# Moving the sums of prepared weight rows from GpSimd to VectorE in a two-layer decoder trunk

## The chip, the cores and the metric

The program runs on one core of one Trainium2 chip. The metric is the device time of one execution in microseconds (us); the lower, the better.

## The reference

The input x is 1024 positions by 1024 features in float32. Layer 0 mixes with an mLSTM (4 heads), layer 1 with sliding-window attention over a shared K/V. Behind each mixer stand an output projection and a SwiGLU feed-forward network, which holds most of the work:

```python
def swiglu(x, w_gate_up, w_down):
    gu = x @ w_gate_up
    g, u = jnp.split(gu, 2, axis=-1)
    return (jax.nn.silu(g) * u) @ w_down
...
x = x + swa_sink_mixer(...)   # or mlstm_mixer, whose last step is h @ w_out
x = x + swiglu(rmsnorm(x, ffn_norm[l]), w_gate_up[l], w_down[l])
```

D_FF is 2816, so that w_gate_up has 1024 x 5632 numbers and w_down 2816 x 1024 in each layer. All of it is float32.

## The kernel before

**Arithmetic.** A float32 number is split into a high part (fp32r) and a low part (the rest), and a product is three matmuls: high by high, high by low, low by high. The large products are also made by a scheme with 7 products of half-sized blocks in place of 8 (NQ = 7). For that, each operand comes in 7 "forms", q = 0 to 6. Some forms are plain blocks b11, b12, b21, b22, others are one of four sums (differences) of blocks: s1 = b12 - b11, s2 = b22 - b12 (written over b12), s3 = b22 - s1, s4 = b21 - s3 (written over b11). Form 1 is split from s1, form 2 from s3, form 4 from s2 and form 6 from s4; forms 0, 3 and 5 need no sum. ScalarE makes the high part of a form (a copy), VectorE the low part (a subtraction, whole form less high part).

**Items.** `run(l)` on each engine walks the items of layer l: 8 "out" items, 22 "up" items (one tile of 128 gate and up columns each; the first of them is plain), 20 "down" items. An item makes 7 products, q = 0 to 6; in an up item each has 12 matmuls. Every engine has a queue of its own, written out by hand in the same loops over items and q, and works through it in order; semaphores join them. The up items with their local numbers 10 to 27 are where this change lies.

**An up item.** TensorE makes product q from the resident forms of x and the matrices `mats`, which come from the streamed weight: GpSimd makes the four sums of the stream two items ahead (`stream_sums`, lines 1068 to 1085), ScalarE the high parts for the next item (L1332), VectorE the low parts of q = 0, 3 and 6 (L1853), GpSimd those of q = 1, 2, 4 and 5 (L1090). The products end in PSUM banks that are used again within the item, so they are emptied at once: ScalarE copies those of q = 0, 1, 2 (L1415, L1420, L1423); VectorE adds those of q = 3, 4, 5 (L1896, L1899, L1902) and makes the two hidden halves at q = 6 (L1908). Product 6 goes into the bank that the addition at q = 4 reads, so TensorE waits for L1899 in front of it:

```python
done, count = ((u_act, 5 * k + 1), (u_act, 5 * k + 3), (u_act, 5 * k + 2), (u_dve, 5 * k + 2)
               )[(2, 4, 5, 6).index(q)]
```

**Preparing rows.** Beside this work the up items prepare the rows of the weights that the following items need (w_down, and layer 1's w_out): 12 rows in layer 0, 11 in layer 1. SyncE loads a row's two raw tiles into one of two buffers (`load_prep`, L826), the four sums are made in place and in two small tiles (`prep_sums`, lines 1044 to 1065), ScalarE makes the high part (`prep_hi_of`, L1311), VectorE the low part (`prep_lo_of`, L1832), and SyncE stores the form in HBM (L831). The table `prep_at` says at which (item, q) a form is made: the 84 or 77 forms of a layer are spread evenly over the 126 products of its items 10 to 27. So in layer 0 forms fall on two of three products, and the pattern repeats every three items:

```python
events = [(runs[l][8 + f].n, q) for f in range(2, 20) for q in range(NQ)]
...
prep_at.setdefault(events[k * len(events) // forms_here], []).append((j0 + k // NQ, k % NQ))
```

In VectorE's queue the order within one q of an up item is: the emptying step (`up_out`), the streamed low parts, the prepared low part.

## Time and profile before

| | us |
|---|---|
| median of 3 runs | 1994.05 (1993.57 to 1995.02) |
| profiled execution | 1993.69 |
| its span | 1991.70 |
| TensorE busy | 1971.0 |
| VectorE busy | 1309.1 |
| ScalarE busy | 921.8 |
| GpSimd busy | 1206.0 |

The span runs from the first to the last instruction on the core; the execution's time is 1.99 us more. Busy times are of one profiled execution. A wait in the profile is put down to the instruction that came last before the waiting one started.

### The profile page before, as it was taken

Reading aid. Unit: us, or ns where it says so; the run is one execution under the profiler, and the core shown is the slowest. Engines: PE = TensorE matmul, PEld = TensorE weight load, DVE = VectorE, ACT = ScalarE, POOL = GpSimd, SP = SyncE. Lnnn points to the kernel's source line nnn. Section 1 sums busy time; section 2 is a strip of 40 time slices with the busy share of each in tenths; the row PEclk is TensorE's granted clock in tenths of the full one; section 3 lists DMA queues with packets and bytes.
Section 4 is the critical chain, followed back from the end, with each engine's and each line's share of the span. In section 5 each row is a group of like instructions: output and inputs, shape, how many; then the busy total and the mean of one; then the engine's idle time right before and its main releaser. Section 6 shows DMA issues by size and latency. Waiting matters only on the chain.

```text
span 1991.7 us, 28791 instructions
## 1 busy us (share of the span) xinstructions
PE 1971.0 (99%) x9987; PEld 1654.9 (83%) x9987; DVE 1309.1 (66%) x1743; ACT 921.8 (46%) x1929; POOL 1206.0 (61%) x1055
## 2 busy tenths in 40 slices
PE   8999999999999999999999999999999999999998
PEld 8898988888888888888888878788888888888886
DVE  6665552688777777564665677779776676645567
ACT  6534333376555555432245465457445444432233
POOL 4443322657988988656664112474988888746566
PEclk9999999999999999999999999999999999999999
DMA  7574545835877778695853123553667757597683
GB/s 209 179 249 169 168 156 208 308 120 169 273 245 240 245 244 254 237 390 186 274 181 75 43 86 107 184 186 117 230 227 231 250 204 263 193 356 265 217 265 132
DMA packets 292627, 414.99 MB, mean 208 GB/s; under 512 B 38128, under 2 KB 215304, under 8 KB 292496
## 3 DMA queue, kind: packets, MB, share of 16 engines
q1 hardware_dynamic: 257792, 307.61, 47.2%
q10 hardware_dynamic: 33280, 100.94, 14.1%
q0 software_dynamic: 1424, 4.77, 0.7%
q8 instruction: 73, 1.20, 0.2%
q14 instruction: 58, 0.48, 0.1%
HBM read 259.09 MB, written 154.17 MB: 207 GB/s over the span
## 4 chain that ended last, share of the span: by engine, by line
PE 89%; DVE 4%; POOL 2%; issue 2%; ACT 1%; DMA 1%; SPq 0%; POOLq 0%; ACTq 0%; DVEq 0%
PE ps L2516 21%; PE ps L2518 21%; PE ps L2517 21%; PE ps L2427 9%; PE ps L2429 5%; PE ps L2892 1%; PE ps L2736 1%; PE ps L2737 1%; PE ps L2733 1%; DVE mats L1853 1%; PE ps L2571 1%; PE ps L2866 1%; DVE forms L1952 1%; PE ps L2777 1%; PE ps L2902 1%
## 5 line engine op out<-in xcount | busy, mean ns | idle before, releaser
L2516 PE MATMUL ps<-forms,mats 128*128 128x512 f32 x2016 | 787.8, 391 | 5.9 <-DVE X L1876 1.8
L2518 PE MATMUL ps<-forms,mats 128*128 128x512 f32 x2016 | 784.9, 389 | 0.0
L2517 PE MATMUL ps<-forms,mats 128*128 128x512 f32 x2016 | 784.6, 389 | 0.0
L1090 POOL TENSOR_TENSOR mats<-sum_a,mats 128x256 fp32r<-128x256 f32 (+2 forms) x384 | 407.3, 1066 | 346.9 <-ACT mats L1332 346.2
L2516 PEld LDWEIGHTS ps<-forms,mats 128*128 128x128 f32 x2016 | 378.5, 188 | 89.5 <-issue 10.2
L2518 PEld LDWEIGHTS ps<-forms,mats 128*128 128x128 f32 x2016 | 378.5, 188 | 78.8
L2517 PEld LDWEIGHTS ps<-forms,mats 128*128 128x128 f32 x2016 | 378.6, 188 | 77.6
L1876 DVE TENSOR_TENSOR X<-ps,X 128x512 f32<-128x512 f32 x390 | 267.9, 689 | 188.6 <-PE ps L2518 186.8
L1332 ACT ACTIVATE mats<-sum_a 128x256 fp32r<-128x256 f32 (+2 forms) x392 | 201.2, 516 | 310.8 <-PE ps L2518 289.5
L1853 DVE TENSOR_TENSOR mats<-stream_raw,mats 128x256 fp32r<-128x256 f32 (+2 forms) x302 | 276.5, 918 | 25.9 <-ACT mats L1332 25.1
L1332 ACT ACTIVATE mats<-stream_raw 128x256 fp32r<-128x256 f32 (+2 forms) x302 | 156.4, 519 | 245.2 <-PE ps L2518 240.4
L1832 DVE TENSOR_TENSOR prep_forms<-prep_raw,prep_forms 128x512 fp32r<-128x512 f32 x115 | 156.2, 1358 | 68.6 <-ACT prep_forms L1311 67.8
L1076 POOL TENSOR_TENSOR sum_a<-stream_raw 128x256 f32<-128x256 f32 (+2 forms) x96 | 112.3, 1170 | 108.7 <-DVE mats L1853 55.9
L2427 PE MATMUL ps<-xT_hi,w_split 128*128 128x512 f32 x400 | 166.4, 416 | 0.0
L2427 PE MATMUL ps<-xT_lo,w_split 128*128 128x512 f32 x400 | 156.2, 391 | 0.0
L2429 PE MATMUL ps<-xT_hi,w_split 128*128 128x512 f32 x400 | 134.4, 391 | 0.0
L1077 POOL TENSOR_TENSOR sum_a<-stream_raw 128x256 f32<-128x256 f32 (+2 forms) x96 | 119.8, 1248 | 0.0
L1081 POOL TENSOR_TENSOR sum_a<-sum_a,stream_raw 128x256 f32<-128x256 f32 (+2 forms) x96 | 115.6, 1205 | 0.0
L1085 POOL TENSOR_TENSOR sum_a<-stream_raw,sum_a 128x256 f32<-128x256 f32 (+2 forms) x96 | 111.0, 1157 | 6.9
L1042 POOL TENSOR_TENSOR raw<-raw,gain_cols 128x1024 f32<-128x1024 f32 x31 | 67.9, 2201 | 38.9 <-DMA raw<-in_b_w_q_dram 17.0
L2427 PEld LDWEIGHTS ps<-xT_hi,w_split 128*128 128x128 f32 x400 | 75.2, 188 | 16.9 <-issue 2.9
L2429 PEld LDWEIGHTS ps<-xT_hi,w_split 128*128 128x128 f32 x400 | 75.1, 188 | 16.4
(268 smaller groups left out, 2619.1 us busy)
## 6 DMA issues: line engine op xcount, KB each, us to landing
forms<-scratch_forms ACTq DMA_DIRECT2D x182, 512.0 KB, 5.4
scratch_forms<-prep_forms SPq DMA_DIRECT2D x161, 512.0 KB, 3.4
stream_raw<-in_w_gate_up_dram SPq DMA_DIRECT2D x88, 512.0 KB, 5.4
scratch_forms<-head_forms SPq DMA_DIRECT2D x49, 512.0 KB, 3.0
scratch_hidden<-hidden SPq DMA_DIRECT2D x84, 256.0 KB, 5.5
prep_raw<-in_w_down_dram SPq DMA_DIRECT2D x38, 512.0 KB, 5.5
stream_raw<-scratch_hidden SPq DMA_DIRECT2D x32, 512.0 KB, 4.8
forms<-scratch_forms SPq DMA_DIRECT2D x28, 512.0 KB, 6.3
```

Of the source, the lines that this page charges most:

```text
L1077: pool.tensor_tensor(s[2], a11, a21, ALU.subtract)
L1081: pool.tensor_tensor(s[1], s[0], a11, ALU.subtract).then_inc(ssum, 2)
L1090: pool.tensor_tensor(blocks(m[:, q, 1, :], it.width), stream_source(it, q), blocks(m[:, q, 0, :].bitcast(F32), it.width), ALU.subtract).th ...
L1332: act.activation(blocks(mats[w][:, q, 0, :], w), stream_source(it, q), ACT.Copy).then_inc(hi_s, 4 if it.plain and q == 3 else 1)
L1832: dve.tensor_tensor(dst[:, 1, :], split_source(prep_raw[j % 2], prep_t, q), dst[:, 0, :].bitcast(F32), ALU.subtract).then_inc(prep_lo, 1)
L1853: dve.tensor_tensor(blocks(m[:, q, 1, :], it.width), stream_source(it, q), blocks(m[:, q, 0, :].bitcast(F32), it.width), ALU.subtract).the ...
L1876: dve.tensor_tensor(xv, ps[:, bank_of(it, q), :], before, ALU.add).then_inc(d_add, 1)
L2427: ms_ = [mm(ps[:, b + half, :], ah, t[:, c[half]], start=start and t is bh, stop=False) for half in halves for t in (bh, bl)]
L2429: ms_ += [mm(ps[:, b + half, :], al, bh[:, c[half]], start=False, stop=stop) for half in halves]
L2516: mm(dst, ah, bh, start=OPENS[q] and k == 0, stop=False, skip_group_check=True)
L2517: mm(dst, ah, bl, start=False, stop=False, skip_group_check=True)
L2518: m = mm(dst, al, bh, start=False, stop=k == w - 1, skip_group_check=True)
```

## The change

`prep_sums` moves from GpSimd's block to VectorE's. The four subtractions, their operands and the semaphore `prep_sum` are as they were; sum 3 now waits for sum 2 of its own row. The places in the queue change too. Before, sums 1 to 3 of a row came in one piece behind the last form of the row in front, and sum 4 behind the row's form 1. Now sums 1, 2 and 3 come one each behind the low parts of forms 4, 5 and 6 of the row in front, and sum 4 behind form 1's. For a layer's first row sum 1 stands at the end of item 9 and sums 2 and 3 behind form 0.

```diff
--- before.py
+++ after.py
@@ -1041,29 +1041,6 @@
                 g = gcol[:, gain_of[u.base], :].unsqueeze(2).to_broadcast([P, KT, P])
                 pool.tensor_tensor(v, v, g, ALU.mult).then_inc(unit_gained, 1)
 
-            def prep_sums(j, these):
-
-                raws, t = prep_raw[j % 2], prep_t
-                b11, b12 = raws[0][:, 0:512], raws[0][:, 512:1024]
-                b21, b22 = raws[1][:, 0:512], raws[1][:, 512:1024]
-                for which in these:
-                    if which == 1:
-                        pool.wait_ge(prep_loaded[j % 2], raw_prep_at[j])
-                        if j:
-                            pool.wait_ge(prep_lo, NQ * (j - 1) + 3)
-                        pool.tensor_tensor(t[0][:], b12, b11, ALU.subtract).then_inc(prep_sum, 1)
-                    if which == 2:
-                        pool.wait_ge(prep_sum, 4 * j + 1)
-                        pool.tensor_tensor(b12, b22, b12, ALU.subtract).then_inc(prep_sum, 1)
-                    if which == 3:
-                        if j:
-                            pool.wait_ge(prep_sum, 4 * j)
-                        pool.tensor_tensor(t[1][:], b22, t[0][:], ALU.subtract).then_inc(prep_sum, 1)
-                    if which == 4:
-                        pool.wait_ge(prep_lo, NQ * j + 1)
-                        pool.wait_ge(prep_sum, 4 * j + 3)
-                        pool.tensor_tensor(b11, b21, t[1][:], ALU.subtract).then_inc(prep_sum, 1)
-
             def stream_sums(it, between=None):
                 w = it.width
                 pool.wait_ge(stream_loaded[stream_buffer(it)], stream_arrived[it.n])
@@ -1133,17 +1110,8 @@
                         for q2 in refill_after(it, q):
                             if not its[i + 1].plain and q2 in SUM_A and not it.plain:
                                 stream_lo(its[i + 1], q2)
-                        for j, form in prep_at.get((it.n, q), []):
-                            if form == 0 and j == preps[l][0].prep:
-                                prep_sums(j, (2, 3))
-                            if form == 1:
-                                prep_sums(j, (4,))
-                            if form == NQ - 1 and j + 1 < end_prep:
-                                prep_sums(j + 1, (1, 2, 3))
                         if i in (6, 7) and 2 <= q < 6:
                             x_form_lo(l, q - 2, i - 6)
-                    if i == 9:
-                        prep_sums(preps[l][0].prep, (1,))
                     if sums_too and not it.seam:
                         stream_sums(its[i + 2])
                     if l == 0 and i == 43:
@@ -1826,6 +1794,28 @@
                                       xh[:, 4 * j:4 * j + 4, t * P:(t + 1) * P].bitcast(F32), ALU.subtract
                                       ).then_inc(bank_free[b], 1)
 
+            def prep_sums(j, these):
+
+                raws, t = prep_raw[j % 2], prep_t
+                b11, b12 = raws[0][:, 0:512], raws[0][:, 512:1024]
+                b21, b22 = raws[1][:, 0:512], raws[1][:, 512:1024]
+                for which in these:
+                    if which == 1:
+                        dve.wait_ge(prep_loaded[j % 2], raw_prep_at[j])
+                        if j:
+                            dve.wait_ge(prep_lo, NQ * (j - 1) + 3)
+                        dve.tensor_tensor(t[0][:], b12, b11, ALU.subtract).then_inc(prep_sum, 1)
+                    if which == 2:
+                        dve.wait_ge(prep_sum, 4 * j + 1)
+                        dve.tensor_tensor(b12, b22, b12, ALU.subtract).then_inc(prep_sum, 1)
+                    if which == 3:
+                        dve.wait_ge(prep_sum, 4 * j + 2)
+                        dve.tensor_tensor(t[1][:], b22, t[0][:], ALU.subtract).then_inc(prep_sum, 1)
+                    if which == 4:
+                        dve.wait_ge(prep_lo, NQ * j + 1)
+                        dve.wait_ge(prep_sum, 4 * j + 3)
+                        dve.tensor_tensor(b11, b21, t[1][:], ALU.subtract).then_inc(prep_sum, 1)
+
             def prep_lo_of(j, q):
                 dst = prep_out[(NQ * j + q) % 2]
                 dve.wait_ge(prep_hi, NQ * j + q + 1)
@@ -2024,6 +2014,12 @@
                             x_form_lo(l, 7, LAST_LO_AT.get(q, ()))
                         for j, form in prep_at.get((it.n, q), []):
                             prep_lo_of(j, form)
+                            if form == 0 and j == preps[l][0].prep:
+                                prep_sums(j, (2, 3))
+                            if form == 1:
+                                prep_sums(j, (4,))
+                            if form >= 4 and j < preps[l][-1].prep:
+                                prep_sums(j + 1, (form - 3,))
                         if l == 0 and i == 44 and q >= 5:
                             key_lo_half(q - 5)
                         if it.seam and it.seam[1]:
@@ -2031,6 +2027,8 @@
                             if q in (2, 5) and norm == 4:
                                 e = q // 4
                                 x_final(pos - 1, its[i - 1].group + 4 * e, e)
+                    if i == 9:
+                        prep_sums(preps[l][0].prep, (1,))
                     if i == 7:
                         for step in (4, 6, 5):
                             x_form_sums(l, step, (2, 3))
```

In the rows below, line numbers of VectorE are 10 smaller in the changed program (L1832 becomes L1822), and the sums stand at L1807, L1810, L1813 and L1817 there. `part_112`, `part_113` and `part_114` are the tiles of the three additions, `mats_62` holds the streamed forms, `prep_raw_97` to `prep_raw_100` are the raw rows, `prep_sum_101` and `prep_sum_102` the two tiles of sums, `prep_forms_103` and `_104` the outputs.

GpSimd's queue at the start of item 10 of layer 0, before and then now:

```order
L1090 TENSOR_TENSOR mats_62<-sum_a_3_78,mats_62 128x512
L1054 TENSOR_TENSOR prep_sum_101<-prep_raw_97 128x512
L1076 TENSOR_TENSOR sum_a_0_75<-stream_raw_64 128x512
L1077 TENSOR_TENSOR sum_a_2_77<-stream_raw_64 128x512
L1081 TENSOR_TENSOR sum_a_1_76<-sum_a_0_75,stream_raw_64 128x512
L1085 TENSOR_TENSOR sum_a_3_78<-stream_raw_64,sum_a_1_76 128x512
L1057 TENSOR_TENSOR prep_raw_97<-prep_raw_98,prep_raw_97 128x512
L1061 TENSOR_TENSOR prep_sum_102<-prep_raw_98,prep_sum_101 128x512
L1090 TENSOR_TENSOR mats_62<-sum_a_0_75,mats_62 128x512
L1065 TENSOR_TENSOR prep_raw_97<-prep_raw_98,prep_sum_102 128x512
```

```order
L1067 TENSOR_TENSOR mats_62<-sum_a_3_78,mats_62 128x512
L1053 TENSOR_TENSOR sum_a_0_75<-stream_raw_64 128x512
L1054 TENSOR_TENSOR sum_a_2_77<-stream_raw_64 128x512
L1058 TENSOR_TENSOR sum_a_1_76<-sum_a_0_75,stream_raw_64 128x512
L1062 TENSOR_TENSOR sum_a_3_78<-stream_raw_64,sum_a_1_76 128x512
L1067 TENSOR_TENSOR mats_62<-sum_a_0_75,mats_62 128x512
L1067 TENSOR_TENSOR mats_62<-sum_a_1_76,mats_62 128x512
```

The four sums of the prepared row (L1054, L1057, L1061, L1065) are out of it, and the streamed matrix's low parts (L1090, now L1067) follow directly on its sums.

VectorE's queue from the end of item 9 of layer 0 into item 10, before and then now:

```order
L1853 TENSOR_TENSOR mats_62<-stream_raw_63,mats_62 128x512
L1853 TENSOR_TENSOR mats_62<-stream_raw_64,mats_62 128x512
L1832 TENSOR_TENSOR prep_forms_103<-prep_raw_97,prep_forms_103 128x512
L1832 TENSOR_TENSOR prep_forms_104<-prep_sum_101,prep_forms_104 128x512
L1896 TENSOR_TENSOR part_112<-ps,part_112 128x512
L1853 TENSOR_TENSOR mats_62<-stream_raw_64,mats_62 128x512
L1832 TENSOR_TENSOR prep_forms_103<-prep_sum_102,prep_forms_103 128x512
L1899 TENSOR_TENSOR part_113<-ps,part_113 128x512
```

```order
L1843 TENSOR_TENSOR mats_62<-stream_raw_63,mats_62 128x512
L1807 TENSOR_TENSOR prep_sum_101<-prep_raw_97 128x512
L1843 TENSOR_TENSOR mats_62<-stream_raw_64,mats_62 128x512
L1822 TENSOR_TENSOR prep_forms_103<-prep_raw_97,prep_forms_103 128x512
L1810 TENSOR_TENSOR prep_raw_97<-prep_raw_98,prep_raw_97 128x512
L1813 TENSOR_TENSOR prep_sum_102<-prep_raw_98,prep_sum_101 128x512
L1822 TENSOR_TENSOR prep_forms_104<-prep_sum_101,prep_forms_104 128x512
L1817 TENSOR_TENSOR prep_raw_97<-prep_raw_98,prep_sum_102 128x512
L1886 TENSOR_TENSOR part_112<-ps,part_112 128x512
L1843 TENSOR_TENSOR mats_62<-stream_raw_64,mats_62 128x512
L1822 TENSOR_TENSOR prep_forms_103<-prep_sum_102,prep_forms_103 128x512
L1889 TENSOR_TENSOR part_113<-ps,part_113 128x512
```

Sum 1 stands in front of the first streamed low part of item 10, and sums 2, 3 and 4 in front of the third addition (`part_112`).

VectorE's queue in item 11 of layer 0, from form 5's low part, before and then now:

```order
L1832 TENSOR_TENSOR prep_forms_103<-prep_raw_97,prep_forms_103 128x512
L1896 TENSOR_TENSOR part_112<-ps,part_112 128x512
L1853 TENSOR_TENSOR mats_62<-stream_raw_63,mats_62 128x512
L1832 TENSOR_TENSOR prep_forms_104<-prep_raw_99,prep_forms_104 128x512
L1899 TENSOR_TENSOR part_113<-ps,part_113 128x512
```

```order
L1822 TENSOR_TENSOR prep_forms_103<-prep_raw_97,prep_forms_103 128x512
L1813 TENSOR_TENSOR prep_sum_102<-prep_raw_100,prep_sum_101 128x512
L1886 TENSOR_TENSOR part_112<-ps,part_112 128x512
L1843 TENSOR_TENSOR mats_62<-stream_raw_63,mats_62 128x512
L1822 TENSOR_TENSOR prep_forms_104<-prep_raw_99,prep_forms_104 128x512
L1889 TENSOR_TENSOR part_113<-ps,part_113 128x512
```

The third sum of the next row now stands between form 6's low part and the third addition; two instructions behind that comes form 0's low part, and then the fourth addition (`part_113`).

## Rows read from the trace of the kernel before

**Rows 1.** The page, part 1: busy time of each engine.
```profile
PE 1971.0 (99%) x9987; PEld 1654.9 (83%) x9987; DVE 1309.1 (66%) x1743; ACT 921.8 (46%) x1929; POOL 1206.0 (61%) x1055
```

**Rows 2.** By stretches: bounds, length, busy us of each engine, granted clock, DMA.
```profile
480.00:780.00 300.00, 299.64 (x1322) 247.88 (x1321) 219.21 (x200) 152.98 (x263) 264.60 (x173) 1.00 0.76 248
1420.00:1740.00 320.00, 318.99 (x1408) 263.94 (x1407) 218.75 (x207) 156.47 (x271) 264.33 (x175) 1.00 0.69 230
```

**Rows 3.** Waits of TensorE, first stretch, then second: us, times, longest.
```profile
PE ps L2516 <- DVE part L1899: 0.4, 1, 0.4
...
PE ps L2516 <- DVE part L1899: 1.4, 2, 1.0
```

**Rows 4.** Timeline, first stop (start us, us, what): third addition, ScalarE, fourth addition, TensorE.
```profile
484.53 0.69 DVE L1896 TENSOR_TENSOR part<-ps,part 128x512 f32<-128x512 f32 x1 [2.26 <-PE ps L2518]
...
487.77 0.63 ACT L1311 ACTIVATE prep_forms<-prep_sum 128x512 fp32r<-128x512 f32 x1 [1.89 <-POOL prep_sum L1061]
...
489.46 0.69 DVE part L1899
...
489.54 0.39 PE L2518 MATMUL ps<-forms,mats 128*128 128x512 f32 x1
...
490.29 0.47 PE L2516 MATMUL ps<-forms,mats 128*128 128x512 f32 x1 [0.36 <-DVE part L1899]
```

**Rows 5.** Timeline, second stop, in layer 1.
```profile
1403.89 0.64 ACT L1311 ACTIVATE prep_forms<-prep_sum 128x512 fp32r<-128x512 f32 x1 [1.91 <-POOL prep_sum L1061]
...
1405.60 0.68 DVE L1899 TENSOR_TENSOR part<-ps,part 128x512 f32<-128x512 f32 x1
...
1406.43 0.47 PE L2516 MATMUL ps<-forms,mats 128*128 128x512 f32 x1 [0.40 <-DVE part L1899]
```

**Rows 6.** Timeline, third stop, in layer 1.
```profile
1653.14 0.63 ACT L1311 ACTIVATE prep_forms<-prep_sum 128x512 fp32r<-128x512 f32 x1 [2.77 <-DMA scratch_forms<-prep_forms]
...
1655.24 0.47 PE L2516 MATMUL ps<-forms,mats 128*128 128x512 f32 x1 [1.01 <-DVE part L1899]
```

**Rows 7.** Groups of the whole span: the first of the four sums on GpSimd.
```profile
L1054 POOL TENSOR_TENSOR prep_sum<-prep_raw 128x512 f32<-128x512 f32 x23 | 38.3, 1667 | 0.0
```

**Rows 8.** The prepared rows' tile: VectorE's low parts, ns min/median/max.
```profile
L1832 DVE TENSOR_TENSOR prep_forms<-prep_raw,prep_forms x115: 677/1361/1801, 478.8 to 1733.6; 128x512 fp32r<-128x512 f32 x115
```

**Rows 9.** Timeline, VectorE and GpSimd both busy.
```profile
571.01 1.78 DVE L1853 TENSOR_TENSOR mats<-stream_raw,mats 128x512 fp32r<-128x512 f32 x1
...
572.71 1.78 DVE L1832 TENSOR_TENSOR prep_forms<-prep_sum,prep_forms 128x512 fp32r<-128x512 f32 x1
...
572.20 1.74 POOL L1077 TENSOR_TENSOR sum_a<-stream_raw 128x512 f32<-128x512 f32 x1
```

**Rows 10.** Timeline, around the first sum of layer 0: VectorE, then GpSimd.
```profile
475.39 1.77 DVE L1853 TENSOR_TENSOR mats<-stream_raw,mats 128x512 fp32r<-128x512 f32 x1
...
478.79 1.78 DVE L1832 TENSOR_TENSOR prep_forms<-prep_raw,prep_forms 128x512 fp32r<-128x512 f32 x1
...
476.58 1.74 POOL L1054 TENSOR_TENSOR prep_sum<-prep_raw 128x512 f32<-128x512 f32 x1
```

**Rows 11.** Timeline, VectorE in a regular item, from the third addition.
```profile
561.57 0.68 DVE L1896 TENSOR_TENSOR part<-ps,part 128x512 f32<-128x512 f32 x1
562.17 1.18 DVE L1853 TENSOR_TENSOR mats<-stream_raw,mats 128x512 fp32r<-128x512 f32 x1
563.47 1.58 DVE L1832 TENSOR_TENSOR prep_forms<-prep_raw,prep_forms 128x512 fp32r<-128x512 f32 x1
564.98 0.68 DVE L1899 TENSOR_TENSOR part<-ps,part 128x512 f32<-128x512 f32 x1
566.77 0.69 DVE L1902 TENSOR_TENSOR part<-ps,part 128x512 f32<-128x512 f32 x1 [1.12 <-PE ps L2518]
```

**Rows 12.** Timeline, GpSimd beside rows 11: a removed sum, its next low part.
```profile
561.06 1.74 POOL L1054 TENSOR_TENSOR prep_sum<-prep_raw 128x512 f32<-128x512 f32 x1
...
566.16 2.67 POOL L1090 TENSOR_TENSOR mats<-sum_a,mats 128x512 fp32r<-128x512 f32 x2
```

## The prediction

> **What bounds the kernel now.** I read the page's busy shares first: TensorE is busy 99% of the span [rows 1]. So only time in which TensorE stands still, or waits for another engine, can be won. The change touches the two stretches in which weight rows are prepared, one in each layer, and the view by stretches is the second thing to read: TensorE is busy 299.64 of 300 us in the one and 318.99 of 320 in the other, with the granted clock at 1.00; VectorE is busy 73% and 68%, GpSimd 88% and 83% [rows 2]. GpSimd is the fuller of the two helpers, which makes the change look sensible, but it is not the bound. The third view, the waits of TensorE, puts the whole idle time down to one line, VectorE's addition at L1899, behind product 4 of an item (the "fourth addition"): once in the first stretch, and the 1.4 us of twice in the second [rows 3]. These three stops are all that is there to win. The fourth view is the timeline around them, which tells who made the addition late.
>
> **What the three stops cost.** TensorE's matmuls follow each other at 0.23 us. At the first stop the last one before it starts at 489.54, so the next was due at 489.77 and starts at 490.29 [rows 4]: 0.52 us. The matmuls behind a stop run up 0.1 us slower, so I call it 0.64. The fourth addition starts 0.83 us before TensorE goes on (489.46 to 490.29 [rows 4], 1405.60 to 1406.43 [rows 5]). The second stop, whose row shows 0.40 us idle to the first one's 0.36, costs about 0.67 us the same way, and the third, with 1.01 [rows 6], about 1.26. In all 2.57 us, 0.13% of the time; with less than 0.2% to win, no outcome on the side of "faster" can be told from none.
>
> The first two have one cause. Both are in the item where the first row of a layer is prepared (item 10). VectorE's addition stands in its queue behind the low part of form 2, that behind ScalarE's high part, and ScalarE waited 1.9 us for GpSimd's third sum, L1061 [rows 4, 5], because GpSimd made four other sums first. The third stop is another thing: ScalarE waited 2.77 us for the store of an earlier form to leave its buffer [rows 6].
>
> **What is removed.** GpSimd loses 4 sums for each of 23 rows, 92 instructions; the first of the four lasts 1.67 us in the mean [rows 7], so 92 are up to 153 us of its 1206 us. TensorE doesn't wait for GpSimd in these stretches [rows 3], so this by itself is worth nothing. What hides it is that GpSimd's low parts of the streamed matrices are made most of an item (19 us) before TensorE reads them.
>
> **What is added.** VectorE gets the same 92 subtractions. No row has them on VectorE; the nearest is its own low part at L1832, with the same shape and both inputs in SBUF: 0.68 us at least, 1.36 in the middle, 1.80 at most [rows 8]. What makes the difference is told by the timeline: when GpSimd has work at the same time, VectorE's and GpSimd's instructions take turns and VectorE's starts come 1.70 us apart (571.01, 572.71) while GpSimd's start at 572.20 and last 1.74 [rows 9]; an addition that reads PSUM keeps its 0.68 us (561.57, [rows 11]). So a moved sum costs VectorE between 0.60 us (its start to the next start, 561.57 to 562.17 for a row of 0.68) and 1.70. Over 92 sums that is 55 to 156 us of VectorE's time, in stretches where it has about 182 us idle [rows 2]. It fits on average, but an average doesn't decide; the queue in front of the fourth addition does. The low end is the likelier: much of the work that GpSimd did beside VectorE were these very sums.
>
> The Trainium skill, page "SBUF — State Buffer", section "Who interferes with whom", says that a VectorE instruction with two SBUF inputs contends with a GpSimd instruction that reads SBUF, and that the one that began first keeps the other out for its whole length. The trace agrees with it (1.70 us apart, against 0.60). By that rule alone a sum that comes behind a GpSimd instruction costs up to 1.70, which is the upper end already taken from the row, and the sum of the prediction would be that of the second rival below.
>
> **The deadline.** In item 10 the third addition waited for TensorE and starts at 484.53, so that is when product 3 ended; the fourth has to start by 489.77 - 0.83 = 488.94, that is 4.41 us behind product 3's end. The other VectorE steps are looser: sums behind forms in the last two products of an item stand in front of the product of the hidden tile, which TensorE needs only two products later through ScalarE's copy.
>
> *Item 10.* The first sum is placed on VectorE at the end of item 9, and it waits for the load of the raw row. GpSimd began it at 476.58 and VectorE's queue reaches it at about 477.1 (475.39 + 1.70) [rows 10], so the data is there and VectorE doesn't stand. Sums 2, 3 and 4 follow in products 0 and 1; form 2's high part is then ready 1.9 us earlier, and the fourth addition starts at about 488 instead of 489.46. Both stops go: 0.64 + 0.67 = 1.31 us won. If all the sums are contended, three of 1.70 and two low parts of 1.70 end at 478.79 + 8.5 = 487.3, the third addition starts 2.8 us late, and the fourth up to 2 us behind its deadline, once for each layer.
>
> *A sum in product 2 and a form in product 3.* This is the tightest of the regular patterns: 6 items of layer 0 and 2 of layer 1. In the item of rows 11 the fifth addition waits for product 5 and starts at 566.77, so product 3 ended 5.44 us before, at 561.33, and the deadline is 565.74. Today the fourth addition starts at 564.98. With the sum in front at 561.57 and nobody beside it, the third addition moves to 562.18; form 0's low part stood 1.90 us behind the third addition (561.57 to 563.47), because ScalarE has to work in between, so it comes at 564.08, and without GpSimd it takes 0.60: the fourth addition starts at 564.68, before today's time. What GpSimd did from 561.06 on were three of the removed sums, and its next low parts come at 566.16 [rows 12].
>
> *A sum in product 3 itself.* Five items of layer 1, none of layer 0. There the sum stands directly in front of the fourth addition, behind a low part that starts about 1.9 us and ends 2.5 us behind product 3: 3.1 with 0.60 and 4.2 with 1.70, both before 4.41. Cost nothing.
>
> *Other queues.* SyncE issues the same DMAs in the same order; a row's load is issued when the last form of the row two in front is stored, five forms (some seven products of 2.7 us) before the new place of its first sum, so no wait on it is added. Between forms the sums come earlier than they did, so ScalarE has nothing new to wait for.
>
> **The sum.** 1993.69 us (span 1991.70 and 1.99 around it) - 0.64 - 0.67 = 1992.4 for the profiled execution. The median of the runs, 1994.05, is 0.36 above it: I forecast 1992.7. The third stop I leave in, as the store isn't touched. About 0.2% (4 us) is what a measurement of this kernel can tell from no change, so the forecast is "no difference".
>
> **Rivals.**
> 1. *The change does nothing at all for the end, or wins all three stops.* For the first: the stop goes to another instruction of the same item. For the second: the 1.26 us of the store wait is a matter of chance. Times: 1994.1 and 1991.5. Both lie within the same bound, and are counted with the forecast.
> 2. *Slower: VectorE is late at the fourth addition.* The mechanism is the turn-taking of rows 9 in the pattern of rows 11: sum 1.70 (to 563.27), third addition 0.60, the streamed low part 1.70 (to 565.57), form 0's low part 1.70, and the fourth addition starts at 567.27, 1.5 us behind 565.74. In 8 items that is 12 us, with some 0.6 us in two of the five items with a sum in product 3 and 2 us in each item 10, 17 us: about 2010. It decides from the point at which GpSimd has work in products 2 and 3. Against it: GpSimd is left without its own sums there. For it: GpSimd's work moves forward, and I know the new places of its low parts only by reasoning. If only part of the items are hit, say two or three, it is 3 to 5 us: 1996 to 1998.
> 3. *Faster by more than 4 us.* It would need a slower pitch of TensorE that is due to GpSimd's reads. No row speaks for it: the pitch is 0.23 us both in and outside the stretches.
>
> **Chances.** Forecast with rival 1: 0.82. Rival 2 in full or for the larger part: 0.15. Rival 3: 0.03. The range reaches down to all three stops won and the runs' own scatter (1991.0), and up to two or three late items (1997.5).
>
> **What would show it.** Right: TensorE's waits on the fourth addition in both items 10 are gone, ScalarE's wait for the third sum too; the moved sums take 0.7 us in products 2 and 3 and up to 1.8 at the start of an item, where GpSimd makes the sums of the streamed matrix; VectorE's low parts get shorter on average than 1.36 us; GpSimd's busy time falls by 150 us or more; TensorE's busy time is unchanged. Wrong: new stops of TensorE behind the fourth addition, in the items with a sum in product 2, repeated every third item of layer 0; or VectorE standing on the load of a raw row.

## The result and the profile after

| | median us | runs | against the kernel before, of the same measurement |
|---|---|---|---|
| before | 1993.55 | 20 | |
| changed | 1996.78 | 20 | 1.0017 (1.0011 to 1.0023) |

The change makes the kernel 3.2 us slower. That lies inside the range that I gave and below the 0.2% (4 us) which I took for the smallest difference that can be told from none; but with 20 runs of each kernel the interval is clear of 1, so that it is a real difference, on the other side of the forecast of 1992.7. The profiled execution took 1996.49 us, with a span of 1994.7 us, 3.0 more than before.

Busy time of each engine, the page's part 1 of the changed kernel (compare [rows 1]):

```profile
PE 1970.8 (99%) x9987; PEld 1654.4 (83%) x9987; DVE 1352.8 (68%) x1835; ACT 920.5 (46%) x1929; POOL 1054.3 (53%) x963
```

TensorE's busy time is as before. GpSimd lost 152 us, and VectorE gained only 44 with 92 instructions more. The 92 sums last 100 us together, but VectorE's other subtractions with both inputs in SBUF got shorter: the 161 prepared low parts by 20 us together (1.34 us in the mean before, 1.22 now), the 310 streamed low parts by 28. By stretches (bounds, length, busy us of PE, PEld, DVE, ACT, POOL, clock, DMA share; compare [rows 2]):

```profile
480.00:780.00 300.00, 297.80 (x1313) 245.93 (x1312) 233.09 (x242) 150.83 (x262) 188.76 (x127) 1.00 0.76 247
1420.00:1740.00 320.00, 319.05 (x1408) 263.86 (x1407) 240.91 (x246) 156.75 (x272) 198.28 (x134) 1.00 0.70 233
```

In the first stretch TensorE is busy 297.80 us where it was 299.64; in the second, which begins behind item 10's stop, there is hardly a difference. Its waits in the changed kernel over the whole span (us, times, longest; compare [rows 3], where the first line had 1.8 us in 3 times and the second didn't exist):

```profile
PE ps L2514 <- DVE part L1889: 3.6, 3, 1.4
...
PE ps L2514 <- ACT part L1383: 0.8, 1, 0.8
```

Where in the span the time went is read from additions that wait for TensorE in both kernels. VectorE's third addition of items 13 and 25 of layer 0, before and then changed:

```profile
542.29 0.69 DVE L1896 TENSOR_TENSOR part<-ps,part 128x512 f32<-128x512 f32 x1 [2.49 <-PE ps L2518]
...
770.77 0.69 DVE L1896 TENSOR_TENSOR part<-ps,part 128x512 f32<-128x512 f32 x1 [1.24 <-PE ps L2518]
```

```profile
543.75 0.69 DVE L1886 TENSOR_TENSOR part<-ps,part 128x512 f32<-128x512 f32 x1 [0.85 <-PE ps L2516]
...
773.37 0.69 DVE L1886 TENSOR_TENSOR part<-ps,part 128x512 f32<-128x512 f32 x1 [0.94 <-PE ps L2516]
```

The distance between the two kernels grows from 1.46 us (542.29 to 543.75) to 2.60 us (770.77 to 773.37). Of the 1.46, 0.52 was there before item 10 (the third addition of item 9 starts at 467.77 before and 468.29 now). So item 10 of layer 0 costs 0.94 more than it did, and something between items 13 and 25 costs 1.14. In layer 1 the distance grows by 0.9 over item 10 (its neighbours: 2.65 at item 9, 3.56 at item 13) and no further to item 24. Together that is about 3 us. What the two executions differ by elsewhere cancels: the 0.52 ahead of item 10 is lost again at the end of layer 1, where the distance falls from 3.5 (third addition at 1764.33 and 1767.85) to the 3.0 of the spans. Two places, then: the two items 10 with 1.8 us, and one stop late in layer 0 with 1.1.

**First place.** Timeline of VectorE in item 10 of layer 0, changed kernel (start us, us):

```profile
477.60 1.79 DVE L1807 TENSOR_TENSOR prep_sum<-prep_raw 128x512 f32<-128x512 f32 x1
479.31 1.77 DVE L1843 TENSOR_TENSOR mats<-stream_raw,mats 128x512 fp32r<-128x512 f32 x1
481.01 1.78 DVE L1822 TENSOR_TENSOR prep_forms<-prep_raw,prep_forms 128x512 fp32r<-128x512 f32 x1
...
486.11 1.77 DVE L1822 TENSOR_TENSOR prep_forms<-prep_sum,prep_forms 128x512 fp32r<-128x512 f32 x1
487.81 0.68 DVE L1817 TENSOR_TENSOR prep_raw<-prep_raw,prep_sum 128x512 f32<-128x512 f32 x1
488.41 0.68 DVE L1886 TENSOR_TENSOR part<-ps,part 128x512 f32<-128x512 f32 x1
...
490.92 0.68 DVE L1889 TENSOR_TENSOR part<-ps,part 128x512 f32<-128x512 f32 x1
```

and GpSimd beside it:

```profile
477.27 1.56 POOL L1053 TENSOR_TENSOR sum_a<-stream_raw 128x512 f32<-128x512 f32 x1
...
483.90 3.43 POOL L1067 TENSOR_TENSOR mats<-sum_a,mats 128x512 fp32r<-128x512 f32 x2
```

VectorE starts seven instructions from 477.60 to 487.81, about 1.70 us apart, beside GpSimd, which works without a gap from 477.27 to 487.33. The third addition starts at 488.41, 3.4 us behind product 3's end (484.53 + 0.52 = 485.05), and the fourth at 490.92, where before it started at 489.46 [rows 4]. What ties the fourth to the third is ScalarE's queue. In it form 2's high part stands behind a copy (L1399) that waits for the third addition:

```profile
489.12 0.63 ACT L1399 ACTIVATE part<-part 128x512 f32<-128x512 f32 x1 [3.44 <-DVE part L1886]
489.66 0.61 ACT L1279 ACTIVATE prep_forms<-prep_sum 128x512 fp32r<-128x512 f32 x1
```

So form 2's high part starts at 489.66, later than the 487.77 of before [rows 4], though the sum that it is made from ends at 486.19 now (484.52 + 1.67). Form 2's low part waits 0.62 us for it, and the fourth addition stands behind that low part. TensorE's stops in the two items 10, where 0.36 and 0.40 stood:

```profile
491.75 0.47 PE L2514 MATMUL ps<-forms,mats 128*128 128x512 f32 x1 [1.35 <-DVE part L1889]
...
1410.01 0.47 PE L2514 MATMUL ps<-forms,mats 128*128 128x512 f32 x1 [1.32 <-DVE part L1889]
```

**Second place.** Around item 23 of layer 0, changed kernel: VectorE's sum 1 and form 5's low part; SyncE's store of it, the load of the streamed matrix behind it, and form 6's store; ScalarE's high part of form 2 some 15 us on; and TensorE:

```profile
727.93 1.78 DVE L1807 TENSOR_TENSOR prep_sum<-prep_raw 128x512 f32<-128x512 f32 x1
...
730.23 1.78 DVE L1822 TENSOR_TENSOR prep_forms<-prep_raw,prep_forms 128x512 fp32r<-128x512 f32 x1
...
732.04 0.32 SPq L831 DMA_DIRECT2D scratch_forms<-prep_forms  x1
...
732.88 0.91 SPq L807 DMA_DIRECT2D stream_raw<-in_w_gate_up_dram  x1
734.49 0.33 SPq L831 DMA_DIRECT2D scratch_forms<-prep_forms  x1
...
747.30 0.63 ACT L1279 ACTIVATE prep_forms<-prep_sum 128x512 fp32r<-128x512 f32 x1 [4.30 <-DMA scratch_forms<-prep_forms]
...
748.56 0.47 PE L2514 MATMUL ps<-forms,mats 128*128 128x512 f32 x1 [0.85 <-ACT part L1383]
```

The same steps before the change (there TensorE doesn't stop):

```profile
728.21 0.68 DVE L1832 TENSOR_TENSOR prep_forms<-prep_raw,prep_forms 128x512 fp32r<-128x512 f32 x1
...
728.91 0.32 SPq L831 DMA_DIRECT2D scratch_forms<-prep_forms  x1
...
729.75 1.05 SPq L807 DMA_DIRECT2D stream_raw<-in_w_gate_up_dram  x1
733.03 0.33 SPq L831 DMA_DIRECT2D scratch_forms<-prep_forms  x1
...
743.35 0.63 ACT L1311 ACTIVATE prep_forms<-prep_sum 128x512 fp32r<-128x512 f32 x1 [1.80 <-DMA scratch_forms<-prep_forms]
```

Take off the 1.47 us by which the kernels differ there. Form 5's low part then ends 1.65 us later (728.89 against 732.01), and its store is issued 1.66 later. That store itself lands no later (it takes 2.7 us from issue to landing, where it took 4.3). But SyncE issues in order, and the load of the streamed matrix stands behind the store in its queue: it is issued 1.67 us later too, takes 6.0 us as before, and so lands that much later. Form 6's store, issued at the same time as before, takes 5.7 us where it took 4.0, and form 0's store 8.3 where it took 6.1. ScalarE makes form 2's high part in the buffer that form 0's store must have left; its wait ends 2.5 us later than before, and its copy for TensorE (L1383) stands right behind. DMAs issued from 725 to 745 us, before and then changed (KB, last column median us to landing):

```profile
scratch_forms<-prep_forms SPq DMA_DIRECT2D x5, 512.0 KB, 4.3
prep_raw<-in_b_w_out_dram SPq DMA_DIRECT2D x4, 256.0 KB, 5.4
```

```profile
scratch_forms<-prep_forms SPq DMA_DIRECT2D x5, 512.0 KB, 5.7
prep_raw<-in_b_w_out_dram SPq DMA_DIRECT2D x4, 256.0 KB, 6.4
```

### The profile page after: what moved, and what is told of

Same layout as the page of the kernel before. It is cut to its first block, busy times and chain, and to the rows that moved or that the text cites. A ratio compares the mean times of both kernels' runs of the same rounds, so it can differ in the third digit from the quotient of the medians.

```text
span 1994.7 us, 28791 instructions
## 1 busy us (share of the span) xinstructions
PE 1970.8 (99%) x9987; PEld 1654.4 (83%) x9987; DVE 1352.8 (68%) x1835; ACT 920.5 (46%) x1929; POOL 1054.3 (53%) x963
## 4 chain that ended last, share of the span: by engine, by line
PE 94%; DVE 3%; issue 1%; ACT 1%; DMA 1%; POOL 0%; SPq 0%; POOLq 0%; ACTq 0%; DVEq 0%
PE ps L2514 22%; PE ps L2515 22%; PE ps L2516 22%; PE ps L2425 9%; PE ps L2427 5%; PE ps L2890 1%; PE ps L2734 1%; PE ps L2735 1%; PE ps L2731 1%; PE ps L2569 1%; PE ps L2864 1%; PE ps L2533 1%; PE ps L2535 1%; PE ps L2534 1%; PE ps L2775 1%
## 5 line engine op out<-in xcount | busy, mean ns | idle before, releaser
L1067 POOL TENSOR_TENSOR mats<-sum_a,mats 128x256 fp32r<-128x256 f32 (+2 forms) x384 | 403.8, 1054 | 504.2 <-ACT mats L1300 504.0
L1843 DVE TENSOR_TENSOR mats<-stream_raw,mats 128x256 fp32r<-128x256 f32 (+2 forms) x302 | 248.1, 826 | 18.9 <-ACT mats L1300 18.3
L1822 DVE TENSOR_TENSOR prep_forms<-prep_raw,prep_forms 128x512 fp32r<-128x512 f32 x115 | 146.2, 1271 | 63.4 <-ACT prep_forms L1279 63.4
L1053 POOL TENSOR_TENSOR sum_a<-stream_raw 128x256 f32<-128x256 f32 (+2 forms) x96 | 106.5, 1110 | 108.9 <-DVE mats L1843 55.9
L1054 POOL TENSOR_TENSOR sum_a<-stream_raw 128x256 f32<-128x256 f32 (+2 forms) x96 | 118.1, 1230 | 0.0
```

Source lines behind the costliest of these rows:

```text
L1054: pool.tensor_tensor(s[2], a11, a21, ALU.subtract)
L1067: pool.tensor_tensor(blocks(m[:, q, 1, :], it.width), stream_source(it, q), blocks(m[:, q, 0, :].bitcast(F32), it.width), ALU.subtract).th ...
L1822: dve.tensor_tensor(dst[:, 1, :], split_source(prep_raw[j % 2], prep_t, q), dst[:, 0, :].bitcast(F32), ALU.subtract).then_inc(prep_lo, 1)
L1843: dve.tensor_tensor(blocks(m[:, q, 1, :], it.width), stream_source(it, q), blocks(m[:, q, 0, :].bitcast(F32), it.width), ALU.subtract).the ...
```

## The experiments

All were made from the changed kernel. A function `sums_at(eng, l, j, form, q)` takes the place of the conditions in the two queues, and says which sums of which row an engine makes behind form `form` of row j in product q; where a sum passes from one engine to the other it waits for the sum in front. `all_here` is the changed kernel's placement, `as_before` that of before. Only the line that differs is shown of each edit. The first row's sum 1 stands at the end of item 9 in every version, on the engine that makes this row's other sums (first_rows_split apart). Each ratio is to the kernel before on the same chip. The stops of TensorE are idle times, read from one profiled execution; a stop of 1.3 us in item 10 makes the kernel 0.9 us slower than the 0.4 of before does.

**control.** The changed kernel as it is.

> The changed kernel again, as the measure for the runs beside it. Expected 3 us above the kernel before (1.0015 to 1.0020 times), with TensorE's two stops of 1.3 to 1.4 us of idle time in the two items 10 and the one of 1.0 us in item 23 of layer 1; the stop of 0.8 us in item 24 of layer 0 may be there or not.

1996.25 us, 1.0013 (1.0004 to 1.0022), 2.6 us above before. Stops in item 10 of 1.32 us twice, 1.26 in item 23 of layer 1, and one of 0.60 behind ScalarE, at 709.33. This last one is another thing than the second place above. No store stands in front of it: ScalarE's copy waits 3.04 us for VectorE's hidden half, and in front of that stands a sum 3 of 1.77 us:

```profile
706.12 1.77 DVE L1813 TENSOR_TENSOR prep_sum<-prep_raw,prep_sum 128x512 f32<-128x512 f32 x1
...
708.58 0.60 ACT L1383 ACTIVATE part<-ps 128x512 f32<-128x512 f32 x1 [3.04 <-DVE hidden L1898]
```

So the changed kernel has two ways to stop TensorE behind ScalarE, and two profiles of it show one each.

**first_rows_gpsimd.**

```diff
-return all_here if eng == "dve" else []
+return [a for a in all_here if (a[0] == first) == (eng == "pool")]
```

> Only the sums of each layer's first row go back to GpSimd, at the places they had before; the other 84 stay on VectorE. Theory 'crowded start' (the queue of five 1.70 us instructions in front of the third addition of item 10 is what costs): both stops in item 10 fall from 1.35 to 0.4 us of idle time, total 1.9 us less than the changed kernel, so about 1 us above the kernel before. Rival 'regular items' (VectorE's extra load costs in many items): no more than 0.5 us less than the changed kernel.

1995.45 us, 1.0009 (1.0000 to 1.0018): 0.8 us below the control, in the profiled spans 2.0 (1992.5 against 1994.5). That is between the two theories (1.9 less, or at most 0.5 less). The stops of item 10 are 0.37 and 0.14 us; a new one of 0.52 stands at the fourth addition of item 11 of layer 0, and the one behind ScalarE stays, 0.87. It is 1.8 us above before, so part of the loss is left: a second cause. The 1.8 overstates its price, as the stop in item 11 isn't in the changed kernel.

**small_stream_sums.**

```diff
+if local(it) == 11:
+    a11, a12, a21, a22 = (v[:, :, 0:8] for v in (a11, a12, a21, a22))
+    s = [v[:, :, 0:8] for v in s]
```

> The changed kernel with GpSimd's four sums of the streamed matrix of local item 11 (made during item 10, beside the first row's sums) cut to 8 of 128 columns of each block; VectorE's queue is the same to the instruction. Theory 'turns': with GpSimd idle there, VectorE's instructions come 0.6 us apart from the second on, the third addition of item 10 is on time, both stops in item 10 are gone, 3.2 us less than the changed kernel. Rival 'queue length' (the four added instructions by themselves are too many in front of the third addition): the stops stay above 0.4 us.

The kernel leaves out 120 of the 128 columns of these sums. 1993.09 us, 0.9999 (0.9990 to 1.0008), 3.2 us below the control, as forecast. Neither item 10 has a stop; the one behind ScalarE stays, 0.64 us. VectorE in item 10 of layer 0:

```profile
476.33 0.74 DVE L1846 TENSOR_TENSOR prep_sum<-prep_raw 128x512 f32<-128x512 f32 x1
...
481.39 0.68 DVE L1856 TENSOR_TENSOR prep_raw<-prep_raw,prep_sum 128x512 f32<-128x512 f32 x1
483.75 0.69 DVE L1925 TENSOR_TENSOR part<-ps,part 128x512 f32<-128x512 f32 x1 [1.68 <-PE ps L2551]
```

The same queue as above: its first seven instructions take from 476.33 to 482.07, 5.7 us, where they took 10.9 (477.60 to 488.49), and the third addition waits for TensorE. So the number of instructions in front of it alone doesn't make it late; GpSimd's work beside them does.

**first_rows_split.**

```diff
+if j == first and form == 0:
+    return [(j, (3,))] if eng == "dve" else [(j, (2,))]
+return as_before if eng == "pool" else []
```

> All sums on GpSimd as before, but sums 1 and 3 of each layer's first row on VectorE (3 directly behind form 0's low part, as it doesn't need sum 2), sums 2 and 4 on GpSimd. Only one of the four sums then stands between form 0 and the third addition. Crowded start and the late third sum of before are both avoided: no stop in either item 10, so 1.3 us below the kernel before (0.9993). If the third addition is late all the same by more than 1 us: no gain.

Here sum 1 stays on VectorE and sum 2 is on GpSimd. 1993.22 us, 0.9998 (0.9989 to 1.0007). No stop in either item 10. VectorE, layer 0:

```profile
483.66 0.68 DVE L1860 TENSOR_TENSOR prep_forms<-prep_sum,prep_forms 128x512 fp32r<-128x512 f32 x1
484.28 0.69 DVE L1924 TENSOR_TENSOR part<-ps,part 128x512 f32<-128x512 f32 x1
...
487.67 0.68 DVE L1927 TENSOR_TENSOR part<-ps,part 128x512 f32<-128x512 f32 x1
```

The third addition is on time, the fourth starts at 487.67. The span is 1989.3 us, 2.4 less than before's, but the median is only 0.4 us below, so it was measured once more:

**split_again.**

> first_rows_split once more, on another chip if so given, as its first look showed no stop in either item 10 but a median only 0.4 us below the kernel before. If the two stops are all it changes: 1.3 us below. If its median is within 0.3 us of before again, something gives the gain back outside the profiled execution.

1992.36 us, 0.9996 (0.9987 to 1.0005), 0.9 us below, where 1.3 was expected. Both medians are lower, neither interval is clear of 1; that it beats the kernel before is likely and not shown.

**late_sums_gpsimd.**

```diff
+return all_here if (q in (4, 5)) == (eng == "pool") else []
```

> The changed kernel, but the sums that fall on products 4 and 5 of an item (30 of the 92) are made by GpSimd at the same places; the first rows stay on VectorE. Theory 'hidden tile late' (a sum behind the low part in product 5 pushes the first hidden half, and so ScalarE's copy that TensorE needs, over its deadline in one item out of several): TensorE's stop on ScalarE's L1383 of 0.6 to 0.9 us in layer 0 is gone, and the first hidden half starts no later than 8.9 us behind the third addition instead of 10.1; 0.7 to 1.1 us less than the changed kernel, the two stops of 1.3 us in item 10 unchanged. Rival 'stores' (a slow store of a form holds ScalarE, whatever VectorE has to do): the stop stays.

1997.39 us, 1.0020 (1.0011 to 1.0030). The stop behind ScalarE stays, 0.83 us, and ScalarE waits 4.28 us for a store in front of it. As the cause of this stop 'hidden tile late' is wrong; it is the cause of the control's.

**first_and_late_gpsimd.**

```diff
+return [a for a in all_here if (a[0] == first or q in (4, 5)) == (eng == "pool")]
```

> Both at once: first rows' sums and those on products 4 and 5 on GpSimd, 54 on VectorE. By the two theories the stops of before alone are left (0.4 in each item 10, about 1 in item 23 of layer 1): within 0.5 us of the kernel before. If removing GpSimd's load or adding to VectorE's has any other price it shows here.

1995.36 us, 1.0009 (1.0000 to 1.0018): not like before; the stop behind ScalarE is 1.07 us, one at the fourth addition of item 11 of layer 0 is 0.50.

**only_first_rows_vector.**

```diff
+return [a for a in as_before if (a[0] == first) == (eng == "dve")]
```

> The complement: all on GpSimd as before, only the first row of each layer (8 sums of 92) on VectorE as in the changed kernel. Crowded start: both stops of 1.3 us, 1.9 us above the kernel before, so 8 sums make two thirds of the loss. Regular items: nothing.

1994.57 us, 1.0008 (0.9999 to 1.0017), 1.6 us above before. Both stops of 1.32 us, none behind ScalarE. It is the complement of first_rows_gpsimd: 1.6 and 1.8 make 3.4 us, where the whole change made 3.2. Each of the two intervals is 3.6 us wide, so the medians alone don't prove the split. The stops agree with it: they are the same (1.32 to 1.35 us) in every kernel with the first rows on VectorE and GpSimd's batch in full beside them.

**three_more_in_product_2.**

```diff
+for _ in range(3):
+    dve.tensor_tensor(prep_t[1][:], prep_raw[row % 2][1][:, 512:1024], prep_t[0][:], ALU.subtract)
```

> The changed kernel with three further copies of sum 3 in front of it on VectorE, only where it stands in product 2 of layer 0 (6 items; each copy waits for the one in front). It measures the margin of the regular items. In the changed kernel the fourth addition starts 3.4 us behind product 3's end and the deadline is 4.4; three copies push it by about 1.8 to 2.1 us, so 0.8 to 1.1 us over it: a stop of about 0.6 to 1 us in each of the 6 items, 5 to 7 us more than the changed kernel. If the margin is larger than I think (VectorE's queue isn't what the addition waits for), nothing.

The copies stand in front of sum 3 where it falls on product 2 of layer 0 (the condition and the semaphores are left out here). 2002.38 us, 1.0047 (1.0033 to 1.0061), 6 us more than the changed kernel. In each of the six items TensorE stops for 0.95 us; VectorE's copies, the fourth addition, and TensorE in one of them:

```profile
562.82 2.13 DVE L2059 TENSOR_TENSOR prep_sum<-prep_raw,prep_sum 128x512 f32<-128x512 f32 x3
...
568.10 0.68 DVE L1926 TENSOR_TENSOR part<-ps,part 128x512 f32<-128x512 f32 x1
...
568.93 0.47 PE L2555 MATMUL ps<-forms,mats 128*128 128x512 f32 x1 [0.95 <-DVE part L1926]
```

0.83 us from the fourth addition to TensorE, as in [rows 4]; the margin of the regular items is as worked out, about 1 us. No stop behind ScalarE stands in this profile.

**start_sums_gpsimd** and **only_start_sums_vector**, a pair: the sums on products 6 and 0.

```diff
+return [a for a in all_here if (a[0] == first or q in (6, 0)) == (eng == "pool")]
...
+return [a for a in all_here if (a[0] != first and q in (6, 0)) == (eng == "dve")]
```

> First rows' sums and those that fall on product 6 or product 0 (where GpSimd makes the streamed matrix's sums and VectorE's instructions come 1.70 us apart) on GpSimd, the others on VectorE. Theory 'late stores' (a sum on VectorE at an item's start puts the next form's low part and its store off by 1.7 us, the stores bunch in SyncE's queue, and ScalarE waits for them): ScalarE's wait for stores of forms falls from 36 us in the three stretches to 16 to 22, the stop of 0.6 to 1.1 us near the end of layer 0's stretch is gone, and the time is within 0.7 us of the kernel before. Rival 'any regular sum on VectorE': waits stay above 28 us and the stop stays, 1.5 us above the kernel before or more.

> The complement: only the sums on products 6 and 0 (first rows apart) on VectorE, the rest on GpSimd. Late stores: ScalarE's waits for stores 28 us or more, the stop of 0.6 to 1.1 us there, 1 to 2 us above the kernel before. Rival: as before, 16 to 20 us of waits and no such stop.

1996.96 us, 1.0020 (1.0010 to 1.0029), and 1995.57 us, 1.0009 (1.0000 to 1.0018). ScalarE's waits for the stores of forms, which were 16 us before the change and are 36 in the changed kernel, are 33 and 31 us, the stop behind it 1.02 and 0.41 (the latter at 518.55, early in layer 0). The first has no sum on VectorE in products 6 and 0, and has the stop all the same: VectorE's part there isn't the cause by itself, and the first half of this theory falls. In both ScalarE's copy stands behind a wait for a store (4.47 and 3.56 us). What both have in common are the new places.

**gpsimd_new_places.**

```diff
+return all_here if eng == "pool" else []
```

> No sum on VectorE at all: GpSimd makes all of them, but the regular rows' sums at the changed kernel's places (behind forms 4, 5, 6 and 1), the first rows' as before. Theory 'engine' (VectorE's part in them shifts the low parts, the stores and so ScalarE): like the kernel before, 20 us or less of ScalarE's waits for stores, no stop of TensorE behind ScalarE, within 0.7 us of before. Rival 'places' (the new places do it, whoever makes the sums): 28 us or more of waits, 1.5 to 2.5 us above before.

1995.28 us, 1.0009 (1.0000 to 1.0018), 1.5 us above before, with no sum on VectorE at all. The stop is there; ScalarE's waits for stores are 25 us, between the bounds that the two theories had (20 and 28). GpSimd's sum 2, form 5's low part, its store, and TensorE (1.56 us, the longest of this kind):

```profile
728.46 1.74 POOL L1067 TENSOR_TENSOR prep_raw<-prep_raw,prep_raw 128x512 f32<-128x512 f32 x1
...
728.98 1.78 DVE L1860 TENSOR_TENSOR prep_forms<-prep_raw,prep_forms 128x512 fp32r<-128x512 f32 x1
...
730.78 0.32 SPq L840 DMA_DIRECT2D scratch_forms<-prep_forms  x1
...
747.55 0.47 PE L2546 MATMUL ps<-forms,mats 128*128 128x512 f32 x1 [1.56 <-ACT part L1420]
```

and the stores issued from 725 to 745 us take as long as in the changed kernel:

```profile
scratch_forms<-prep_forms SPq DMA_DIRECT2D x5, 512.0 KB, 5.7
```

**vector_old_places.**

```diff
+return [a for a in as_before if (a[0] == first) == (eng == "pool")]
```

> Regular rows' sums on VectorE, but at the places of before (three in one piece behind form 6, the fourth behind form 1), first rows on GpSimd. 'Engine': 28 us or more of waits for stores, and 1.5 us or more above the kernel before; the three in one piece in product 2 of layer 0 put the fourth addition some 1.2 us later than one does, so small stops there as well (6 items, up to 0.4 us each). 'Places': no stop behind ScalarE.

2004.49 us, 1.0052 (1.0039 to 1.0066). ScalarE's waits for stores are 14 us, about as before the change, the longest 2.3; form 5's low part in item 23 takes 0.68 us again (at 736.03), and no stop comes from a store. The theory 'engine' falls. The absence of the stop alone would not show it, as TensorE stands still 11 us more in this kernel and the DMAs have that much more time. The 11 us are another thing: three sums in one piece at the end of an item, each about 1.70 us, in front of the hidden tile, which makes ScalarE's copy late and stops TensorE for 1.03 us in each of 5 items (the way of the control's stop), and for 0.2 to 0.75 us at the fourth addition of six others; in layer 1 there are two more at the fourth addition, of 0.23 and 0.98 us. VectorE's sum 1, the hidden half and ScalarE's copy:

```profile
532.46 1.78 DVE L1845 TENSOR_TENSOR prep_sum<-prep_raw 128x512 f32<-128x512 f32 x1
...
537.56 0.68 DVE L1936 TENSOR_TENSOR hidden<-ps,part 128x512 f32<-128x512 f32 x1
...
538.33 0.60 ACT L1420 ACTIVATE part<-ps 128x512 f32<-128x512 f32 x1 [5.00 <-DVE hidden L1936]
```

## Why the prediction was wrong

The sum took off 0.64 and 0.67 us, for the two items 10, and put nothing on. The profiles show 0.94 and 0.9 us more there, and 1.1 more at a stop behind ScalarE that the sum had at nothing.

**Item 10** is the step that failed first. It said that both stops go, 1.31 us won, with the fourth addition at about 488. It came at 490.92. Two things were wrong in it. The price of a moved sum was taken at the low end, 0.60 us, with the argument that GpSimd is left without its own sums. That holds for the stretch between two batches of stream sums, not at an item's start, where those four and the low parts behind them fill GpSimd (477.27 to 487.33); there the instructions come 1.70 us apart. And "form 2's high part is then ready 1.9 us earlier" followed the sum alone: in ScalarE's queue the copy that waits for the third addition stands in front of it, and with the third addition late it came 1.4 us later than before (489.66 against 487.77 + 0.52), not 1.9 earlier. small_stream_sums shows that GpSimd's work there is what decides, and only_first_rows_vector prices the place: 8 of the 92 sums make about half of the loss.

The text had the other end too: "the third addition starts 2.8 us late, and the fourth up to 2 us behind its deadline, once for each layer". That is near what happened: 3.4 us late, and the fourth 1.5 us behind its deadline (490.92, against 488.94 + 0.52), a stop that costs 0.9 us more in each layer than the one of before. The 2.8 was too small, as its sum starts form 0's low part at 478.79, where it stood before, though sum 1 now comes in front of it; it starts at 481.01.

**The regular items** were right for the changed kernel. In the items with a sum in product 2 the fourth addition starts 2.5 us behind the third. The low parts and the sums last at least 0.68 us and at most 1.79; the low parts' median is unchanged at 1.36, their mean fell:

```profile
L1822 DVE TENSOR_TENSOR prep_forms<-prep_raw,prep_forms x115: 677/1361/1784, 481.0 to 1737.1; 128x512 fp32r<-128x512 f32 x115
...
L1807 DVE TENSOR_TENSOR prep_sum<-prep_raw x23: 676/685/1787, 477.6 to 1696.9; 128x512 f32<-128x512 f32 x23
```

No regular item has a new stop at the fourth addition, and three_more_in_product_2 confirms the deadline. The margin is thin in item 11 of layer 0, though: with the first rows on GpSimd and other sums on VectorE it had a stop there of 0.50 to 0.59 us in three kernels. Rival 2, which put 17 us on the regular items and item 10, had the right place in item 10 and the wrong one in the rest.

**Other queues** is the second step that failed: "ScalarE has nothing new to wait for". It has the stores, whose waits rose from 16 to 36 us. I followed the loads and the semaphores of the sums, and not when the low parts end and with them the stores. The sums' new places, one by one behind forms 4, 5 and 6, put contended instructions in front of form 5's low part, or beside it, at an item's start. The wait comes with either engine: gpsimd_new_places has the long wait and the stop, vector_old_places has neither. I had costed both edits, the engine and the places, as one.

A third step failed in the control alone: that the sums in an item's last two products are in front of "the product of the hidden tile, which TensorE needs only two products later", and so are looser. The control's profile shows TensorE 0.60 us idle behind just that, and three in one piece (vector_old_places) 1.03 us.

**The third stop** stays, 0.95 us where it was 1.01 [rows 6], as the prediction had it; in the experiments it lies between 0.44 and 1.86, and why it varies wasn't looked into. "TensorE's busy time is unchanged", the fall of GpSimd's busy time by 150 us, and the removed work being worth nothing were right as well. The bound from above was right too: there was little to win, with 2.57 us of stops in all.

**What stays open.** The streamed matrix's load and a hidden tile's store (256 KB) stand behind form 5's store and are issued later by as much as the low part, and what is issued next lands about as much later. That this pushes the stores is argued from these times; no run moves the load alone. Nor is it known why form 0's store then takes 8.3 us in the changed kernel and 8.6 in gpsimd_new_places, but 6.4 in three_more_in_product_2 with the same issue times up to form 6's store. Nor is the stop behind a store in every profile: it is at 519 in only_start_sums_vector, at 745 to 749 in most, and not in the control, which is the same kernel as the changed one, nor in three_more_in_product_2. It costs 1.1 us in the changed kernel's profile and 1.8 in that of gpsimd_new_places (from 0.26 us ahead of the kernel before to 1.54 behind), whose median is 1.5 above.

## What to carry to other kernels

Moving work from a helper engine that isn't the bound to another wins nothing by the work removed, and its price is set where the two engines run side by side: cost the moved instructions at the contended time wherever the other engine has a batch, start-up items first, rather than at the mean. When a change moves both the engine and the place of a step, cost them apart, and follow the finish times down to the stores, to what stands behind them in the issuing queue, and to whoever waits for a buffer to be stored. Where the bounds of one step straddle its deadline, the end for the worse belongs in the forecast if nothing in the rows shows the other engine idle there.

## What the runs showed of the hardware

A VectorE subtraction of 128x512 with both inputs in SBUF took 0.68 us beside an idle GpSimd and 1.78 us when GpSimd had instructions back to back, at starts 1.70 us apart; additions that read PSUM stayed at 0.68 to 0.69. The Trainium skill, page "SBUF — State Buffer", section "Who interferes with whom", states that a VectorE instruction with two SBUF inputs contends with a GpSimd instruction that reads SBUF; the runs agree, and small_stream_sums shows it with VectorE's queue held fixed. What I hadn't expected is the size of it in one place: the same seven instructions took 10.9 us beside GpSimd's full batch and 5.7 us beside the small one.

SyncE issued in order: with a store held back by 1.66 us for its low part, the load behind it went 1.67 us later. In five profiles (before, changed, gpsimd_new_places, vector_old_places, three_more_in_product_2) the load went 0.84 us behind the store, whenever that was.
